# GpSimd makes the low parts of the activation sums; four other steps are moved in their queues

## The reference, cut to what matters

```python
# first block, the part behind the mixer
h = rms_norm(x, norm2_g)
gate, val = jnp.split(h @ w_up, 2, axis=-1)          # 1024 -> 2 x 2816
gate = jax.nn.silu(causal_depthwise_conv(gate, ffn_dw_w, ffn_dw_b))
x = x + (gate * val) @ w_down                        # 2816 -> 1024
# second block
u = rmsnorm(x, norm_mix_w)
proj = u @ w_in_2                                    # mixer: recurrent heads and sliding-window heads
...
v = rmsnorm(h, norm_ffn_w)
gate = causal_depthwise_conv_2(v @ w_gate, conv_w, conv_b)
h = h + (jax.nn.silu(gate) * (v @ w_up)) @ w_down
return rmsnorm(h, final_norm_w)
```

## Time and profile before

| | |
|---|---|
| time, median of 3 runs | 1188.14 us (1187.74 to 1188.22) |
| the profiled execution, its own time | 1186.67 us |
| its span, first to last instruction | 1184.9 us |
| mean granted TensorE clock | 0.997 |
| busy: TensorE / weight loads | 1150.5 us / 995.0 us |
| busy: VectorE, ScalarE, GpSimd | 842.7, 627.4, 592.4 us |

### The profile page before, as it was taken

One profiled execution on the slowest core, in us unless ns is written; L12 is line 12 of the kernel. 1 busy time (PEld: TensorE's weight loads), 2 busy tenths in 40 slices (PEclk: granted clock), 3 DMA queues, 4 the chain that ended last, 5 costly groups with the idle time before them and its releaser, 6 DMA issues.

```text
span 1184.9 us, 19193 instructions
## 1 busy us (share of the span) xinstructions
PE 1150.5 (97%) x7668; PEld 995.0 (84%) x7668; DVE 842.7 (71%) x1103; ACT 627.4 (53%) x1007; POOL 592.4 (50%) x308
## 2 busy tenths in 40 slices
PE   7999999989999999999999999999999999999997
PEld 6877767779999998888867777778899999988886
DVE  5998974389888887544575587943898888885444
ACT  6346585545656564322555646656556565643323
POOL 3650132646767675544683210018457676755443
PEclk9999999999999999999999999999999999999999
DMA  6689671744866766636432211213234343432221
GB/s 184 239 218 221 187 210 28 177 138 159 207 204 204 201 223 197 185 142 157 119 93 95 71 37 38 73 36 108 89 107 144 116 151 108 150 126 84 104 89 71
DMA packets 110786, 162.64 MB, mean 137 GB/s; under 512 B 3587, under 2 KB 90986, under 8 KB 110698
## 3 DMA queue, kind: packets, MB, share of 16 engines
q1 hardware_dynamic: 97738, 115.02, 29.8%
q0 software_dynamic: 12800, 46.14, 15.8%
q10 hardware_dynamic: 160, 0.26, 0.1%
HBM read 159.05 MB, written 48.23 MB: 175 GB/s over the span
## 4 chain that ended last, share of the span: by engine, by line
PE 84%; DVE 8%; ACT 3%; issue 2%; POOL 2%; DMA 1%; SPq 0%; POOLq 0%; DVEq 0%; ACTq 0%
PE ps L2373 31%; PE ps L2424 10%; PE ps L2428 10%; PE ps L2039 6%; PE ps L2040 6%; PE ps L2041 6%; PE ps L2128 4%; PE ps L2612 4%; PE ps L2174 1%; PE ps L2564 1%; PE ps L2159 1%; DVE sum_raw L1637 1%; DMA w_raw<-in_w_in 1%; POOL w_lo L662 1%; DVE cv L1616 1%
## 5 line engine op out<-in xcount | busy, mean ns | idle before, releaser
L662 POOL TENSOR_TENSOR w_lo<-w_raw,w_hi 128x1024 fp32r<-128x1024 f32 x176 | 460.4, 2632 | 277.2 <-ACT w_hi L796 275.9
L796 ACT ACTIVATE w_hi<-w_raw 128x1024 fp32r<-128x1024 f32 x210 | 220.9, 1054 | 192.6 <-PE ps L2428 77.2
L2373 PE MATMUL ps<-tt,w_hi 128*128 128x256 f32 x1280 | 233.8, 284 | 3.5 <-DVE act_t L1663 3.1
L2373 PEld LDWEIGHTS ps<-tt,w_hi 128*128 128x128 f32 x1280 | 200.9, 193 | 3.9 <-issue 3.3
L2373 PE MATMUL ps<-tt,w_lo 128*128 128x256 f32 x640 | 181.8, 284 | 0.0
L1605 DVE TENSOR_TENSOR tt<-act_t,tt 128x512 fp32r<-128x512 f32 x44 | 103.7, 2367 | 101.9 <-ACT tt L1021 101.9
L2039 PE MATMUL ps<-h_hi,w_hi 128*128 128x512 f32 x376 | 152.9, 407 | 3.7 <-DVE h_lo L1395 1.2
L2040 PE MATMUL ps<-h_lo,w_hi 128*128 128x512 f32 x376 | 146.9, 391 | 0.0
L2041 PE MATMUL ps<-h_hi,w_lo 128*128 128x512 f32 x376 | 146.8, 390 | 0.0
L2373 PE MATMUL ps<-h_lo,w_hi 128*128 128x256 f32 x440 | 124.5, 283 | 0.0
L2373 PE MATMUL ps<-h_hi,w_hi 128*128 128x256 f32 x440 | 124.5, 283 | 0.0
(11 more groups left out here) (334 smaller groups left out, 2264.1 us busy)
## 6 DMA issues: line engine op xcount, KB each, us to landing
blocks<-in_w_up POOLq DMA_DIRECT2D x28, 1408.0 KB, 10.4
w_raw<-in_w_up SPq DMA_DIRECT2D x40, 512.0 KB, 3.5
w_raw<-blocks SPq DMA_DIRECT2D x40, 512.0 KB, 3.6
w_raw<-in_w_in SPq DMA_DIRECT2D x19, 1024.0 KB, 5.1
w_raw<-in_w_down SPq DMA_DIRECT2D x18, 1024.0 KB, 4.8
w_raw<-in_w_gate SPq DMA_DIRECT2D x20, 512.0 KB, 3.5
w_raw<-in_w_out SPq DMA_DIRECT2D x8, 1024.0 KB, 5.6
blocks<-in_w_gate POOLq DMA_DIRECT2D x4, 1408.0 KB, 6.8
```

Source lines behind the costliest of these rows:

```text
L662: pool.tensor_tensor(unit_view(w_lo, at, flat), unit_raw(at, flat), unit_view(w_hi, at, flat).bitcast(F32), ALU.subtract).then_inc(s_lo, 1)
L796: act.activation(unit_view(w_hi, at, flat), unit_raw(at, flat), ACT.Copy).then_inc(s_hi, 1)
L2373: mm = pe.matmul(ps[:, bank, 0:NH], weight[:, k, n], a, start=begin, stop=False, skip_group_check=True)
```

## The change

Six edits. (1) `cross_lo` leaves VectorE; GpSimd makes the four low parts of each network in one run, behind the low part of unit `u0 + 3` and ahead of the first `sevenfold`'s units. (2) `cross` 1 waits for four tiles of `xg` instead of eight and goes ahead of the wait for the statistics, `cross` 2 goes between `variance` and `spread`. (3) `split_lo(lay, 1)` moves from ahead of the fourth `joined` of the last `sevenfold` to behind both `lower`. (4) `raw_lo(6)` and `raw_lo(7)` move from behind `spread(3)` to ahead of the wait for the statistics. (5) ScalarE's `lead(U_IN2 + 4)` moves from behind `norm_hi` to between its fourth and fifth tile. (6) GpSimd's low part of that unit moves from behind `cmask` and `band` to ahead of them. No product and no byte of transfer is added or removed.

```diff
@@ -726,9 +726,16 @@
...
                 add_squares(n, 7)
 
+            def cross_lo(lay, n):
+                x = (0, 1, 3, 2)[n - 1]
+                pool.wait_ge(s_th, 4 * lay + n)
+                pool.tensor_tensor(t_lo[x], t_f[x], t_hi[x].bitcast(F32), ALU.subtract).then_inc(s_tl, 1)
+
             projected(1, U_OUT + 4)
             inverse_root(2)
             rests(U_UP + 3, 1)
+            for x in range(1, 5):
+                cross_lo(0, x)
             rests(U_UP + 4, U_IN2 + 2 - U_UP - 4)
             for m in range(1, KD):
@@ -752,6 +759,7 @@
...
                 link(pool.affine_select(out=upper, in_=upper, compare_op=ALU.is_ge, fill=0.0, base=m - 1,
                                         pattern=[[2 * m, n], [0, m]], channel_multiplier=-1))
+            rests(U_IN2 + 4, 1)
             link(pool.memset(cmask[:], 1.0))
             link(pool.memset(cmask[:, 0:SEQ:P], 0.0))
@@ -761,7 +769,7 @@
...
                                     pattern=[[-1, P]], channel_multiplier=1))
             assert steps[1] == GC
-            rests(U_IN2 + 4, 14)
+            rests(U_IN2 + 5, 13)
 
             for j in range(1, 4):
@@ -769,6 +777,8 @@
...
             inverse_root(8)
             rests(U_UP2 + 3, 1)
+            for x in range(1, 5):
+                cross_lo(1, x)
             rests(U_UP2 + 4, U_DOWN2 - U_UP2 - 4)
             rests(U_DOWN2, 22)
@@ -821,8 +831,10 @@
...
             lead(3)
 
-            def norm_hi(n):
+            def norm_hi(n, u=None):
                 for k in range(KD):
+                    if k == 4 and u is not None:
+                        lead(u)
                     act.wait_ge(s_ht, k + 1)
                     act.activation(h_hi[:, k, :], htmp[:, k % 2, :], ACT.Copy).then_inc(s_hhi, 1)
@@ -1130,7 +1142,7 @@
...
             ffn(0, U_UP, C_FB)
             down(0, 2, U_DOWN, True)
-            norm_hi(2)
+            norm_hi(2, U_IN2 + 4)
 
 
@@ -1141,7 +1153,6 @@
...
                 act.activation(out_ap, in_ap, func, **kw).then_inc(s_take2, 1)
 
-            lead(U_IN2 + 4)
             act.wait_ge(s_kv, 2)
             take(0, kT[:, 0, :], ps[:, 0, :], ACT.Identity, bias=bias(4))
@@ -1561,9 +1572,10 @@
...
                 b21, b22 = xg[:, KH:KD, 0:NH], xg[:, KH:KD, NH:SEQ]
                 if n == 1:
-                    dve.wait_ge(s_xg, KD * (lay + 1))
+                    dve.wait_ge(s_xg, KD * lay + KH)
                     dve.tensor_tensor(t1f, b11, b12, ALU.subtract).then_inc(s_tf, 1)
                 if n == 2:
+                    dve.wait_ge(s_xg, KD * (lay + 1))
                     dve.wait_ge(s_tf, 4 * lay + 1)
                     dve.scalar_tensor_tensor(t2f, b22, -1.0, t1f, ALU.mult, ALU.subtract).then_inc(s_tf, 1)
@@ -1572,19 +1584,16 @@
...
                     dve.tensor_tensor(t3f, b22, b12, ALU.subtract).then_inc(s_tf, 1)
 
-            def cross_lo(lay, n):
-                x = (0, 1, 3, 2)[n - 1]
-                dve.wait_ge(s_th, 4 * lay + n)
-                dve.tensor_tensor(t_lo[x], t_f[x], t_hi[x].bitcast(F32), ALU.subtract).then_inc(s_tl, 1)
-
             def norm_later(n, rb_n, gcol, lay):
 
                 gain_lo(n, gcol, range(1, KD))
+                cross(lay, 1)
                 dve.wait_ge(s_stat, STATS[n] + 1)
                 variance(ps[:, 4, 0:TT], DM)
+                cross(lay, 2)
                 spread(rb_n)
-                for x in range(1, 5):
-                    cross(lay, x)
+                cross(lay, 3)
+                cross(lay, 4)
                 dve.wait_ge(s_rb, rb_n)
                 dve.tensor_copy(rbs[:], ps[:, 5, :]).then_inc(s_rbs, 1)
@@ -1654,7 +1663,6 @@
...
                         half_sum(NC[lay], 0)
                         half_sum(NC[lay], 1)
-                        cross_lo(lay, 1)
                     for c in range(2):
                         wait_used(dve, u0 + 4 * i + 2 + c)
@@ -1691,9 +1699,7 @@
...
                                                  cv[:, c, :], ALU.mult, ALU.mult).then_inc(s_gv, 1)
 
-                    if first:
-                        cross_lo(lay, 2)
-                    else:
+                    if not first:
                         half_sum(i, 1)
                     rest(u + 3)
@@ -1701,14 +1707,10 @@
...
                             dve.wait_ge(s_gv, KF * lay + 2 * i + c - 1)
                         joined(c, 2, q1c, q1_at, left, CROSS)
-                    if first:
-                        cross_lo(lay, 3)
-                        cross_lo(lay, 4)
                     if not last:
                         half_sum(i + 1, 0)
                     else:
                         split_lo(lay, 0)
-                        split_lo(lay, 1)
                     for c in range(2):
                         joined(c, 4, q6c, 4, right, SUM)
@@ -1719,6 +1721,7 @@
...
                         lower(0)
                         lower(1)
+                        split_lo(lay, 1)
                         gated(0)
                         gated(1)
@@ -1753,16 +1756,14 @@
...
                     if m in RAW_LO:
                         raw_lo(RAW_LO.index(m))
-                raw_lo(4)
-                raw_lo(5)
+                for k in range(4, KD):
+                    raw_lo(k)
 
             ffn(0)
...
             variance(ps[:, 4, 0:TT], DM)
             spread(3)
-            raw_lo(6)
-            raw_lo(7)
             normalize(2, 3, C_NM, 5)
             dve.wait_ge(s_scaled, 4 * NUP)
```

## The result

The changed kernel takes 1181.29 us (median; 1180.33 to 1182.27) beside 1188.0 us for the kernel before in the same comparison: a ratio of 0.9948, 95% interval 0.9936 to 0.9961. It is faster by 6.7 us, where 4.15 were forecast. The profiled execution took 1182.27 us (span 1180.5 and 1.8 around it), 4.4 us less than the 1186.67 us of before's. So the sum, which was made against the profiled execution, is met within 0.3 us; the other 2.3 us lie between the two profiled executions and their medians (before's profiled execution was faster than every one of its timed runs, after's was the slowest of its own).

The account below looks back on a forecast made before the run. TensorE, busy 97% of 1184.9 us, bounds the kernel, so only its waits and low clock can be won. Terms -1.2, +0.5, -1.85, -1.85, +0.25 sum to -4.15 us: 1182.5 profiled, 1184.0 median; range 1178.5 to 1188.8.

Parts of the forecast that it names:

- How Vector and GpSimd share: A Vector instruction with two SBUF inputs and a GpSimd one exclude each other; the waiting one gets the next turn.
- The first and second rival: Vector keeps the port between back-to-back instructions, 1180.1 us, chance 0.15; no exclusion at all, 1172.3 us, chance 0.03.
- First network's start, -1.2: From 236 to 285 us: TensorE's overhead falls from 6.9 to 5.65 us, -1.2 us; bounds 0 and -6.9.
- the new wait: First network's start: TensorE waits 3.6 us from 253.7 for GpSimd's low part for the first product.
- the 0.4 us for the fourth product: First network's start: the fourth product waits 0.4 us for a Vector low part.
- "Free" for the first sum: First network's start: `cross` 1 moves into an idle stretch before the statistics at no cost.
- Second network's start, +0.5: TensorE waits 2.4 us for `rbs` near 842, later waits vanish: +0.5 us; bounds -3.3 and +2.1.
- Ends of the networks, -1.85 twice: Moving `split_lo(1)` removes TensorE's 1.74 us wait at each network's end: -1.85 us, twice; bounds 0 and -1.95.
- Second mixer, +0.25: Earlier normalization gains 0.75 us, but the moved low part delays Vector, unit 4 starts later: +0.25 us; bounds -1.9 and +0.5.
- The collision: Second mixer: Vector's seventh `h_lo` asks at 605.62 and waits until 607.75 for GpSimd's moved low part.
- the third rival: The clock also falls after the new waits at `rbs` (2.4 us) and in the mixer (2.0): 1187.0 us, chance 0.15.
- fourth rival: TensorE stays at the lower clock longer, three low stretches costing 3.3 us each: 1192.2 us, chance 0.10.

Follow-up runs that it names:

- the run of order and split: Kernel before with the new order of the four sums and `split_lo(lay, 1)` behind the joins, low parts still on Vector: 1182.60 us, ratio 0.9958.
- the split alone: Kernel before with one edit, `split_lo(lay, 1)` moved behind the joins in both networks: 1183.87 us, ratio 0.9971.
- the last placement: Spread low parts without the mixer's lead and early low part, GpSimd's first two low parts moved behind Vector's fourth sum: 1174.29 us, ratio 0.9893.
- The run beside it: The last placement with the mixer's lead and early low part put back as in the changed kernel: 1175.62 us, ratio 0.9895.

## Why the prediction was right, step by step

- **How Vector and GpSimd share** carried the sum and held: 3.40 and 3.42 us for the third and fourth sums, 11.87 for GpSimd's four, and 1.21 each once GpSimd only wrote. It holds as a rule of exclusion; that the one that waited always gets the next turn fails in one place (last section). The first and second rival fall. By the median alone the first, 1180.1 us, is nearer to 1181.29 than the forecast's 1184.0, but what it says did not happen: the third and fourth sums were held, and TensorE waited for `rbs`.
- **First network's start, -1.2:** measured -2.0. The mechanism was right (a new wait for GpSimd's low part, the old one for `act_t` and the two behind it gone). The terms that were mis-sized are the new wait, 2.84 us and not 3.6, and the 0.4 us for the fourth product, which did not come. "Free" for the first sum was wrong by a little: it met GpSimd's sum of squares, which took 2.77 us and not 1.31, TensorE waited 0.47 us for that at 237.13, and the variance came at 238.22 and not 237.88. The same meeting in the second network (2.76 and not 1.64 us, a wait of 0.22 at 828.24) is most of the +0.3 that the table has there; the run of order and split has it too, the split alone doesn't.
- **Second network's start, +0.5:** the offset moved by -0.1. The wait for `rbs` is there with 1.87 us (forecast 2.4), with the wait for the transposes behind it (1.32 us at 850.87) and none at 876.
- **Ends of the networks, -1.85 twice:** measured -2.2 and -2.1 in the profiles, 3.65 for both in the run of that edit alone.
- **Second mixer, +0.25:** the mechanism and the price held; the term that failed is the fall of the clock, put at nothing. The collision came as told: GpSimd's low part at 601.13 and the seventh `h_lo` held to 604.66.

```profile
601.32 3.34 DVE L1406 TENSOR_TENSOR h_lo<-htmp,h_hi 128x512 fp32r<-128x512 f32 x2
...
601.13 2.37 POOL L662 TENSOR_TENSOR w_lo<-w_raw,w_hi 128x1024 fp32r<-128x1024 f32 x1
```

  The forecast's 2.0 us wait came as 1.76. TensorE's first wait ended 0.9 us earlier (0.75 forecast), lead and low part took 0.9 us (1.0 forecast), together nothing with the clock at 1.00, in four profiles. What makes +1.65 of it in the profiled execution is the fall alone, 1.6 us. This is half of the third rival, which held its chance of 0.15 for a fall behind both new waits; the fall behind `rbs` did not come.
- **From the profiled execution to the median.** The forecast carried the 1.47 us between before's profiled execution and its median over to the changed kernel. After's profiled execution was 1.0 above its median instead, so the median fell 2.7 us below the 1184.0 forecast while the profiled time was met within 0.3. The second set of runs of the changed kernel has its median at 1182.84. That the carried 1.47 us came out with the other sign is why the median's forecast is worse than the sum's. An offset of one execution is not a property of a kernel.
- **Slower (fourth rival):** the lower level lasted under 4 us each time but one (from 257.4 to 260.7 in the changed kernel), and two falls in one profile was the most seen; no run was slower than before. It falls. One low stretch was as long as it feared, though, from 257.3 to 264.1 in the second profile of the changed kernel, and that start took 1.1 us more than the first profile's.

What stays open: the size of the two medians' difference between the changed kernel's two sets of runs (1181.29 and 1182.84, each with its own before at 1188.0 and 1187.71); and how much taking the low parts off Vector is worth in the placement of the change. All edits but the mixer's against order and split: 1181.71 and 1182.60, on different chips, 0.7 us apart by their distances from the kernel before, within their intervals; the profiles of the two starts say 0.5.

## What to carry to other kernels

Before work goes from Vector to GpSimd, look at what Vector runs in that stretch: beside instructions on PSUM the moved work cost nothing here, beside ones with two SBUF inputs it gave back most of its gain. Keeping the two apart was worth some 7 us more (1181.15 to 1174.29), in two steps: 2.5 for spreading the low parts, 4.3 for a wait behind the sums and the order that goes with it. A low part nobody needs yet, ahead of an instruction that somebody waits for, was worth 3.65 us when moved behind it, more than the move between the engines in the changed kernel's placement. And price a stall at the reader's clock with and without a fall, as two cases, not as one.

## What the runs showed of the hardware

- **The same wait and two clocks.** Behind a wait of 1.76 us the granted clock fell in one execution of the kernel (0.74 and 0.69) and stayed at 1.00 in another. In the profiles it fell after waits of 3.15, 2.84, 2.81, 2.80, 2.26, 2.05 and 1.86 us and not after 2.60, 2.59, 1.93, 1.90, 1.87, 1.79 and 1.78. Once it fell behind 0.92 us, in the run of one edit alone, ahead of all edits; the other eleven profiles have that wait, 0.93 us, without a fall:

```profile
140.44 0.47 PE L2128 MATMUL ps<-w_hi,h_hi 128*128 128x512 f32 x1 [0.92 <-DVE qk L1452]
...
142.00:144.00 2.00, 2.00 (x6) 0.50 0.14 24
```

  So the length of a wait alone doesn't tell whether it costs itself or itself and a fall; the fall cost 1.56 us in the kernel before and 1.6 in the mixer.
- **Turns are not strict.** `sum_raw` of the last placement (shown above) began at 253.51 and took 6.54 us: it began 0.07 us into GpSimd's issue of a DMA, and two GpSimd subtractions of 4.77 us in all ran ahead of it undisturbed. The run beside it shows the same, 6.53 us at 253.58. In the kernel before, the same instruction, begun 0.41 us into a subtraction of GpSimd's, took 3.10 us and came between the two. That the DMA issue is the cause was not tried.
- **A wait ahead of all edits moved by itself.** TensorE waited 0.32 us for an `h_lo` at 230.88 in one profile of the changed kernel and 1.66 us at 232.81 in another; in the first GpSimd's low part there began at 227.87, in the second at 229.81. It was 0.53 to 0.67 us in three of the other profiles and 1.59 to 1.90 in seven. A difference of 1 us between two profiles of this kernel needs its place before it is put down to an edit.
